# Two transformer blocks at fp32 precision on one core: where token tiles begin relative to the weight tiles in SBUF

## The reference

```python
# first block
y = hybrid_mixer(x, w_in, ...)       # projections of x, a sparse and a full attention, two gates
#   merged = sigmoid(ga) * (o_a @ w_o_dsa) + sigmoid(gb) * (o_b @ w_o_moba);  y = merged @ w_out
x = layer_norm(ALPHA * x + y, ...)
y = mem_cross_attention(x, mem, w_q, w_kv, w_o)   # 256 memory tokens
x = layer_norm(ALPHA * x + y, ...)
y = (silu(g) * u) @ w_ffn_out        # g, u = x @ w_ffn_in, hidden width 5632
x = layer_norm(ALPHA * x + y, ...)
# second block
p = modulate(rms_norm(x)) @ w_in_2   # Fourier part, mLSTM queries, keys, values, gates
x = x + gate1 * (concat(fourier, mlstm) @ w_out_2)
x = x + gate2 * ((silu(a) * v) @ w_down_2)        # a, v = conv(modulate(rms_norm(x)) @ w_up_2)
out = rms_norm(x)
```

## Time and profile before

| | |
|---|---|
| median of 3 runs | 2550.38 us (2550.28 to 2550.78) |
| span of the profiled execution | 2547.0 us |
| TensorE busy (matmuls) | 2493.2 us, 98% |
| VectorE, ScalarE busy | 1671.7 us (66%), 1243.8 us (49%) |
| chain that ended last | TensorE 96%, of it line 2015 61% and line 2058 22% |

### The profile page before, as it was taken

The page is one execution under the profiler, slowest core; times in us unless marked ns, Lnnn a source line. Parts: engine busy times, 40 slices in busy tenths (PEclk is TensorE's granted clock), DMA queues, the critical chain, the costliest instruction groups (busy, mean ns, idle before and its releaser), DMA issues.

```text
span 2547.0 us, 45703 instructions
## 1 busy us (share of the span) xinstructions
PE 2493.2 (98%) x17896; PEld 2329.8 (91%) x17896; DVE 1671.7 (66%) x2081; ACT 1243.8 (49%) x1581; POOL 105.7 (4%) x149
## 2 busy tenths in 40 slices
PE   8999999999989999999999979999899999999998
PEld 8799999998979999999988878988899999998886
DVE  5564675457867777777777775575756566665556
ACT  5444554444564434444444554545555555554444
POOL 0000000000100000000122000000000000000000
PEclk9999999999999999999999989999999999999999
DMA  7455445569647888888978635445355555555553
GB/s 288 166 184 191 156 148 187 191 242 360 257 150 293 330 341 333 343 331 340 357 294 318 263 122 214 168 158 208 144 199 190 190 196 194 188 195 213 187 194 116
DMA packets 81633, 581.92 MB, mean 228 GB/s; under 512 B 9261, under 2 KB 9421, under 8 KB 11409
## 3 DMA queue, kind: packets, MB, share of 16 engines
q1 hardware_dynamic: 64800, 462.98, 49.4%
q0 software_dynamic: 14464, 104.23, 10.5%
q10 hardware_dynamic: 2288, 13.59, 1.4%
HBM read 578.64 MB, written 2.12 MB: 228 GB/s over the span
## 4 chain that ended last, share of the span: by engine, by line
PE 96%; DVE 3%; ACT 1%; issue 0%; DMA 0%; ACTq 0%; DVEq 0%
PE ps L2015 61%; PE ps L2058 22%; PE ps L2019 7%; PE ps L2105 2%; PE ps L1971 1%; PE ps L2083 0%; PE ps L2340 0%; DVE xn L1525 0%; PE ps L2181 0%; DVE res L1530 0%; PE ps L2214 0%; PE ps L2226 0%; DVE wlo L1137 0%; DVE res L1670 0%; DMA xT<-in_xt 0%
## 5 line engine op out<-in xcount | busy, mean ns | idle before, releaser
L1137 DVE TENSOR_TENSOR wlo<-raw,whi 128x1024 fp32r<-128x1024 f32 x860 | 1041.5, 1227 | 663.6 <-ACT whi L592 659.9
L592 ACT ACTIVATE whi<-raw 128x1024 fp32r<-128x1024 f32 x860 | 900.6, 1060 | 964.5 <-PE ps L2015 599.0
L2015 PE MATMUL ps<-xhi,whi 128*128 128x256 f32 x4176 | 1158.4, 277 | 5.4 <-issue 5.4
L2015 PE MATMUL ps<-xlo,whi 128*128 128x256 f32 x4176 | 1152.3, 276 | 0.0
L2015 PE MATMUL ps<-xhi,wlo 128*128 128x256 f32 x4176 | 1152.2, 276 | 0.0
L2015 PEld LDWEIGHTS ps<-xhi,whi 128*128 128x128 f32 x4176 | 787.0, 188 | 7.5 <-issue 6.5
L2015 PEld LDWEIGHTS ps<-xlo,whi 128*128 128x128 f32 x4176 | 787.1, 188 | 0.4
L2015 PEld LDWEIGHTS ps<-xhi,wlo 128*128 128x128 f32 x4176 | 786.8, 188 | 0.0
L1189 DVE SCALAR_TENSOR_TENSOR ada<-ada,cb 128x2048 f32<-128x2048 f32 x96 | 219.4, 2285 | 5.2 <-DMA ada<-in_w_ada 5.2
L2058 PE MATMUL ps<-wlo,dhi 128*128 128x512 f32 x624 | 192.2, 389 | 0.0
L2058 PE MATMUL ps<-whi,dhi 128*128 128x512 f32 x624 | 192.1, 389 | 0.0
(11 more groups left out here) (356 smaller groups left out, 2121.2 us busy)
## 6 DMA issues: line engine op xcount, KB each, us to landing
raw<-in_stream SPq DMA_DIRECT2D x437, 1024.0 KB, 4.8
ada<-in_w_ada POOLq DMA_DIRECT2D x96, 1024.0 KB, 6.9
xT<-in_xt SPq DMA_DIRECT2D x4, 512.0 KB, 6.0
mem_part<-in_memt ACTq DMA_DIRECT2D x2, 1024.0 KB, 7.0
res<-in_x ACTq DMA_DIRECT2D x1, 2048.0 KB, 14.5
gamma<-in_ln_g ACTq DMA_DIRECT2D x2, 1024.0 KB, 9.9
beta<-in_ln_b ACTq DMA_DIRECT2D x2, 1024.0 KB, 14.2
gate_row<-gate_store POOLq DMA_DIRECT2D x2, 1024.0 KB, 6.1
```

The lines of the kernel that those rows point to most:

```text
L592: act.activation(whi[:, h % 4], raw[g % 4][:, 1024 * half:1024 * half + 1024], ACT.Copy)\
L1137: dve.tensor_tensor(wlo[:, h % 4], raw[g % 4][:, 1024 * half:1024 * half + 1024], whi[:, h % 4].bitcast(F32), ALU.subtract).then_inc(lo_re ...
L2015: ins = pe.matmul(o, w[:, k, P * m:P * m + P], a(kt), start=begins and n == 0 and m % 2 == 0, stop=ends and n == 2, skip_group_check=True)
```

## The change

It changes where tiles begin in SBUF, and nothing in what is computed. No instruction changes its place on an engine; one memset on GpSimd is gone, with the unused tile `zeros`, and the counts of `built` that others wait for are one less.

| tiles | used as | bytes past the base before | after |
|---|---|---|---|
| ohi, olo (attention outputs) | moving (T) | 64 | -16 (112 modulo 128) |
| mhi, mlo (memory tokens) | moving (T), stationary (N) | 64 | -16 |
| ckhi, cklo (latents) | moving (T), stationary (N) | 64 | -16 |
| sets 1 and 3 in xhi (xlo: 256 more) | both | 112 | 112 |
| set 2 (q_mem) | moving (T) | 112 | 16 |
| set 4 (lstm_*, fourier) | both | 112 | 120 |
| set 5 (up2) | moving (T) | 112 | 96 |
| shi, slo, hid, dhi, dlo, more_hi, more_lo | wide products | 0 | 0 |
| other pool tiles (fp32 data, not split) | | 64 | 128 (qk: -16) |

```diff
-SHIFT = 64
+SHIFT = 128
+BEHIND = 16
 APART = 256
-SKEW = [(112,)] * 6
+SKEW = [(112,), (112,), (16,), (112,), (120,), (96,)]
...
-        xhi = sb("xhi", [P, KT * S + 112 // 4], F32R)
+        xhi = sb("xhi", [P, KT * S + 128 // 4], F32R)
...
-        qk = sb("qk", [P, 32, S], F32, at_pool)
-        ohi = sb("ohi", [P, 16, S], F32R, at_pool)
-        olo = sb("olo", [P, 16, S], F32R, at_pool + 16384)
+        def behind(name, blocks, at, dt=F32R):
+            lead = (32 - BEHIND) // 4
+            tile = sb(name, [P, lead + blocks * S], dt, at - 32)
+            return tile[:, lead:lead + blocks * S].rearrange("p (k t) -> p k t", t=S)
+
+        qk = behind("qk", 32, at_pool, F32)
+        ohi = behind("ohi", 16, at_pool)
+        olo = behind("olo", 16, at_pool + 16384)
...
-        mhi = sb("mhi", [P, KT, S], F32R, at_pool)
-        mlo = sb("mlo", [P, KT, S], F32R, at_pool + 16384)
+        mhi = behind("mhi", KT, at_pool)
+        mlo = behind("mlo", KT, at_pool + 16384)
...
-        zeros = sb("zeros", [P, 512], BF16)
...
-        ckhi = sb("ckhi", [P, 2, S], F32R, at_pool + 8192)
-        cklo = sb("cklo", [P, 2, S], F32R, at_pool + 10240)
+        ckhi = behind("ckhi", 2, at_pool + 8192)
+        cklo = behind("cklo", 2, at_pool + 10240)
...
-            pool.memset(zeros[:], 0.0).then_inc(built, 1)
```

More of the change, by code:

```diff
@@ L144, in two_blocks @@
         at_xhi = place[0]
-        xhi = sb("xhi", [P, KT * S + 112 // 4], F32R)
+        xhi = sb("xhi", [P, KT * S + 128 // 4], F32R)
         at_xlo = at_xhi + 4 * KT * S + APART
         place[0] = at_xlo
-        xlo = sb("xlo", [P, KT * S + 112 // 4], F32R)
+        xlo = sb("xlo", [P, KT * S + 128 // 4], F32R)
         at_res = place[0]
@@ L484, in _ @@
             pool.memset(ones[:], 1.0).then_inc(built, 1)
-            pool.memset(zeros[:], 0.0).then_inc(built, 1)
             pool.memset(expo[:], -0.5).then_inc(built, 1)
             pool.memset(causal[:], 0.0).then_inc(built, 1)
-            pool.wait_ge(built, 5)
+            pool.wait_ge(built, 4)
             pool.affine_select(out=ident[:], in_=ident[:], compare_op=ALU.not_equal, fill=1.0, base=0,
@@ L495, in _ @@
                 pool.iota(iota_i[:, c0:c1], pattern=[[1, c1 - c0]], base=-q0, channel_multiplier=-1).then_inc(built, 1)
-            pool.wait_ge(built, 10)
+            pool.wait_ge(built, 9)
             pool.tensor_copy(dist[:], iota_i[:]).then_inc(built, 1)
@@ L515, in ada_turns @@
                         pool.wait_ge(ada_used, at(n0 + s - 1, i, per))
-                        pool.wait_ge(built, 11)
+                        pool.wait_ge(built, 10)
                         pool.dma_start(ada[s % 2][:], w_ada[at(n0 + s, i, per)]).then_inc(ada_landed[s % 2], 16)
@@ L538, in _ @@
             pool.memset(lv[:, :, :, DV:DV + 2], 1.0).then_inc(built, 1)
-            pool.wait_ge(built, 13)
+            pool.wait_ge(built, 12)
             for d, st, t0, t1, c0 in BLOCKS:
@@ L810, in sqrt_table @@
             def sqrt_table():
-                act.wait_ge(built, 11)
+                act.wait_ge(built, 10)
                 act.activation(scratch(0, 4), ones[:, 0:1], ACT.Sqrt)
@@ L1003, in _ @@
                     if n == 3:
-                        act.wait_ge(built, 13)
+                        act.wait_ge(built, 12)
                     for t in range(T):
@@ L1203, in _ @@
             dve.wait_ge(weights_used, through(g0 + 2))
-            dve.wait_ge(built, 11)
+            dve.wait_ge(built, 10)
             order.mark(dve.tensor_copy(kw[:], ps[:, 0:2, LATENT:wide_n]))
@@ L1842, in _ @@
                     dve.wait_ge(g_cols, 1)
-                    dve.wait_ge(built, 17)
+                    dve.wait_ge(built, 16)
                 else:
@@ L2156, in _ @@
                 if s == 2:
-                    pe.wait_ge(built, 6)
+                    pe.wait_ge(built, 5)
                     pe.wait_ge(ck_ready, 2)
```

## The result

The changed kernel takes 2577.93 us (median of 4 runs, 2577.42 to 2578.82) against 2550.33 us, a ratio of 1.011 with a 95% interval of 1.0098 to 1.0121. It is slower by 27.6 us, where 5.7 us less was forecast and the range ended at 2559.

The account below looks back on a forecast made before the run. The prediction took the pace of TensorE's matmuls as the only bound. Its terms, -4.4 for moving pool tiles and -1.3 for set 4, summed to -5.7 us: 2544.7 us beside 2550.38, range 2532 to 2559.

Parts of the forecast that it names:

- The step that failed: Set 5's 4224 moving matmuls, 112 to 96 bytes: stay at 113.4 ns, 0 us; bounds +18.6 and -23.7 us.
- The sentence that 113.4 "looks like a floor": Set 5: 112 bytes already matches the wide products' pace per column with tokens at 0, so no gain was taken.
- The rival that set 5 gets slower: Up2's moving tokens at 96 pay 117.8 ns as at 64: +18.6 us there, 2563.3 us in all; chance 0.20.
- The first term: Attention outputs, memory tokens and latents as moving operands, 1008 matmuls, go from 117.8 to 113.4 ns: -4.4 us.
- The rival that their halves must be 256 bytes apart: Attention outputs stay slow because their halves share a place modulo 1024: first term 0, 2549.1 us; chance 0.08.
- Stationary memory tokens and latents: 120 matmuls with these tiles as stationary operands stay at 233.4 ns: 0 us, bound -0.8 us.
- Set 4: lstm_* and fourier, 112 to 120 bytes: moving 0 us (bounds +3.6, -4.6), stationary -1.3 us, half the step.
- Set 2: q_mem's 192 moving matmuls, 112 to 16 bytes: 0 us; bounds +0.8 and -1.1 us.
- Writers, memset, fp32 tiles: Writes of the moved tiles, the removed memset and fp32 tiles moved 64 bytes: 0 each; fp32 loss bound +2.6 us.
- the bound of 107.8 ns: Lowest pace allowed for 256 moving columns, read from fp32 product L2265 as two passes over 256 columns.
- The 3.4 us around the span: Time outside the profiled 2547.0 us span, added to the forecast span of 2541.3 us to reach the forecast time.
- line of 16 bytes: SBUF line rule set against the first term: 64 and 112 cost the same, only set 4 touches one line more.

Follow-up runs that it names:

- the ramps: Two runs of the changed kernel with the 16 blocks of sets 4 and 5 at different offsets, every 8 bytes, then finer near 112: 2577.8 and 2573.2 us.

## Why the prediction was wrong

**The step that failed** is set 5, "By the nearest row it stays at 113.4 and costs 0". It cost 6.6 ns on each of 4224 matmuls, 27.9 us. Three things were wrong in it. I ranked places by their distance in bytes and allowed at most a slope between 64 and 112, but there is no slope: of the places tried 112 alone is good, and 108 and 116, at 118 to 122 ns, are as bad as 64. I took support from the wide products with tokens at 0, where the tokens are the stationary operand; as moving operand tokens at 0 go at 119.9 ns and not at 113.3. And I called 117.8 ns, the row at 64, the upper bound, which 120.0 exceeds. A row at one other address bounds nothing here. The sentence that 113.4 "looks like a floor" held: nothing ran below it. But a floor met at one tested place says nothing of how wide it is. The rival that set 5 gets slower had the right sign and got 0.20, for a reason that fell (96 paying as 64 does, being near it); with 120.0 for its 117.8 ns it would have given 27.9 us for set 5.

**The first term held.** Attention outputs, latents and memory tokens went from 117.8 to 113.4 ns, as the same place suggested; 4.4 us were forecast and 3.3 measured in the run with the sets at 112, with 4.4 inside the interval; k_mem's share of 0.8 us goes into other waits. The place was even nearer than the prediction said: not 112 modulo 128 only, but 112 modulo 1024. The prediction took 112 modulo 128 as enough, which the tokens at 240 contradict; that it came out right there is luck. The rival that their halves must be 256 bytes apart fell: they lie at one place modulo 1024 and run at 113.4.

**Stationary memory tokens and latents** stayed at 233 ns, as said. **Set 4** was mis-sized on both sides. Form N at 120 took nearly the full step, 43.63 / 192 = 227.2 ns, -2.4 us where I took half. Form T at 120 went to 11.52 / 96 = 120.0 and above, +5.4 us and more where I took 0 and bounded it at 3.6, by the same wrong upper row. **Set 2** cost 0.6 us, within its bounds, but the pace that it was given (0, from stationary tokens at 0) was the wrong one. **Writers, memset, fp32 tiles** cost nothing that shows; the pieces that hold none of the moved fp32r tiles kept their lengths.

**Readings that were off.** The fp32 product L2265 has eight matmuls (four heads, two blocks of queries) and sixteen rows. So a matmul of 256 columns leaves two rows of 215.6 ns and takes 431 ns, which is four times 107.8 and not twice; the bound of 107.8 ns is then a quarter of a matmul, and keeps its size. The 3.4 us around the span are too much, as said above. And the chances of faster and same were 0.43 and 0.37, rounded to 0.44 and 0.36. None of these touches the step that failed.

**The Trainium skill's line of 16 bytes** ("SBUF — State Buffer", specifications) does not tell these places apart. By it 96 and 112 are alike, since both begin on a line, and the trace has 120.0 beside 113.4 ns. The estimate of 109.2 ns for 256 columns, from the Trainium skill's page "TensorE: Matmul & The Clock Gate" (Wait — 56ns, not 53.3ns?), was not reached by any fp32r stream in any run here.

**What stays open.** That streams collide and fall into a rhythm is the reading of steps that repeat every two, five or six matmuls at wrong places and every one at 112. What collides with what is not shown. The next operand's load does not explain the runs, the own one in step with the whole train is not excluded, and form N has other good places (0, 120 and, by its 43.62 us, 240) than form T.

## What to carry to other kernels

Where the pace of back-to-back fp32r matmuls matters, treat the distance between the stationary and the moving tile as a tuned constant, measured in steps of 4 to 8 bytes for each form of product, and don't interpolate between two measured values. Blocks of one stage at different offsets map sixteen values in one profile; confirm the winner with a whole set, since neighbours blur it by one to two ns and in one case by eight. Anything inserted ahead of such a tile (padding, another tile) moves the distance, and the control of an address experiment must keep it.

## What the runs showed of the hardware

- Form T (256 moving columns) against the tokens' place past the weights, a whole set at one place: 0 bytes 119.9 ns, 16 bytes 116.7 or 118.7, 64 117.8, 96 120.0, 112 113.4, 120 about 120 to 121, 240 117.2. Nothing else in the ramps was below 116 but blocks at 112.
- Form N (512 columns): 0 bytes 227.4, 120 227.2, 240 227.2, 112 and 64 233.4 to 233.5.
- A common shift of 32 bytes changes nothing (462.71 us in both pieces); a shift of one of four operands by 128 bytes (`xlo` 117.8 ns, `wlo` 118.2) costs 4 to 5 ns in the mean of the three passes.
- The pace did not depend on what VectorE, ScalarE and the DMA queues did at the time, at the good place (113.4 ns in up1 and up2) or at a bad one (120.0 in both).
- fp32 products: L2270 keeps 3.45 us for 16, as before, but both its tiles moved by 64 bytes and their distance stayed, so it tells nothing of places. In the attention scores beside gate_a (`qk` moving past `qs`) the distance did change, `qk` going from 64 to 112 bytes, and the rows of 256 columns still follow each other at 218 ns. That is one pair of places; no more was tried.
